# Layer 0's attention scores from rounded high and low parts of Q and K

## What is computed

```
aq, ak, av, bq, bk, bv = _split_even(hx @ w_in)          # tokens
caq, cak, cav, cbq, cbk, cbv = _split_even(hc @ w_in)    # context
aq = _apply_rope(aq, cos, sin);  ak = _apply_rope(ak, cos, sin)
ya = _window_attn(aq, ak, av, cak, cav, sink)            # band, and a sink
yb = _neighbourhood_attn(bq, bk, bv, cbk, cbv, rpb)      # bias table
y_c = concat([_ctx_attn(caq, cak, cav, sink), _ctx_attn(cbq, cbk, cbv, None)]) @ w_out
# each: s = (q . k) * 64 ** -0.5 (+ bias);  p = softmax(s);  out = p . v
```

## Time and profile before

| | us |
|---|---|
| median of 3 runs | 1332.49 |
| lowest, highest | 1331.76, 1337.83 |
| the profiled execution | 1336.08 |
| its span, first to last instruction | 1334.2 |

### The profile page before, as it was taken

The page is one execution under the profiler, slowest core; times in us unless marked ns, Lnnn a source line. Parts: engine busy times, 40 slices in busy tenths (PEclk is TensorE's granted clock), DMA queues, the critical chain, the costliest instruction groups (busy, mean ns, idle before and its releaser), DMA issues.

```text
span 1334.2 us, 25050 instructions
## 1 busy us (share of the span) xinstructions
PE 1298.1 (97%) x9434; PEld 1151.0 (86%) x9434; DVE 988.5 (74%) x1734; ACT 668.2 (50%) x1358; POOL 195.1 (15%) x268
## 2 busy tenths in 40 slices
PE   7999999999999999999999999999999999999997
PEld 6786779988888888898896899999999988999967
DVE  5698778999887878979428665655666886765884
ACT  4427743631523414344237664565465566465573
POOL 0101223000000000123104610000220016120043
PEclk8999999999999999999999999999999999999999
DMA  7774124366885867934320245655575443455511
GB/s 298 292 214 149 49 82 156 139 221 220 320 311 208 297 238 264 309 125 155 111 80 17 68 162 173 228 181 168 157 264 174 144 130 105 156 175 176 175 51 48
DMA packets 67665, 233.15 MB, mean 175 GB/s; under 512 B 7280, under 2 KB 12400, under 8 KB 67312
## 3 DMA queue, kind: packets, MB, share of 16 engines
q1 hardware_dynamic: 67568, 231.84, 51.6%
HBM read 230.76 MB, written 1.05 MB: 174 GB/s over the span
## 4 chain that ended last, share of the span: by engine, by line
PE 82%; DVE 7%; issue 3%; ACT 3%; POOL 2%; DMA 2%; SPq 0%; ACTq 0%; POOLq 0%; DVEq 0%
PE ps L1722 23%; PE ps L1723 23%; PE ps L1724 23%; PE ps L1947 4%; PE ps L1976 3%; PE ps L2007 2%; DVE wlo L969 2%; DMA aring<-aall 2%; POOL RS L1599 1%; PE ps L1991 1%; DVE ps L1043 1%; DVE ps L1006 1%; ACT whi L611 1%; DVE X L1389 1%; ACT wk L731 1%
## 5 line engine op out<-in xcount | busy, mean ns | idle before, releaser
L969 DVE TENSOR_TENSOR wlo<-raw,whi 128x1024 fp32r<-128x1024 f32 (+1 forms) x284 | 346.3, 1221 | 146.2 <-ACT whi L611 140.7
L611 ACT ACTIVATE whi<-raw 128x1024 fp32r<-128x1024 f32 (+1 forms) x284 | 296.5, 1045 | 262.7 <-PE ps L1724 260.5
L1722 PE MATMUL ps<-H,whi 128*128 128x256 f32 (+1 forms) x896 | 300.5, 335 | 3.9 <-DVE wlo L969 1.6
L1723 PE MATMUL ps<-H,whi 128*128 128x256 f32 (+1 forms) x896 | 296.9, 331 | 0.0
L1724 PE MATMUL ps<-H,wlo 128*128 128x256 f32 (+1 forms) x896 | 296.8, 331 | 0.0
L1722 PEld LDWEIGHTS ps<-H,whi 128*128 128x128 f32 x896 | 169.1, 189 | 24.3 <-issue 5.7
L1724 PEld LDWEIGHTS ps<-H,wlo 128*128 128x128 f32 x896 | 169.3, 189 | 16.9
L1723 PEld LDWEIGHTS ps<-H,whi 128*128 128x128 f32 x896 | 169.2, 189 | 16.1
L1722 PE MATMUL ps<-HID,whi 128*128 128x256 f32 (+1 forms) x536 | 175.3, 327 | 0.0
L1723 PE MATMUL ps<-HID,whi 128*128 128x256 f32 (+1 forms) x536 | 175.1, 327 | 0.0
L1724 PE MATMUL ps<-HID,wlo 128*128 128x256 f32 (+1 forms) x536 | 175.1, 327 | 0.0
(11 more groups left out here) (266 smaller groups left out, 2058.2 us busy)
## 6 DMA issues: line engine op xcount, KB each, us to landing
raw<-wall SPq DMA_DIRECT2D x270, 512.0 KB, 4.2
aring<-aall SPq DMA_DIRECT2D x144, 512.0 KB, 4.8
raw<-wall SPq DMA_DIRECT2D x14, 384.0 KB, 3.0
AL<-ali SPq DMA_DIRECT2D x14, 192.0 KB, 5.4
X<-xin SPq DMA_DIRECT2D x2, 1024.0 KB, 7.2
BI<-rpb SPq DMA_DIRECT2D x4, 512.0 KB, 9.2
out<-X SPq DMA_DIRECT2D x4, 256.0 KB, 2.4
cst<-const SPq DMA_DIRECT2D x1, 960.0 KB, 8.3
```

The costliest lines, as they stand in the source:

```text
L611: act.activation(whi[:, slot, 0:n], raw[:, slot, 0:n], ACT.Copy).then_inc(sem("w_hi"), 1)
L969: dve.tensor_tensor(wlo[:, slot, 0:n], raw[:, slot, 0:n], whi[:, slot, 0:n].bitcast(F32), ALU.subtract)\
L1722: pe.matmul(o, a[0], b[0], start=first, stop=False)
L1723: pe.matmul(o, a[0], b[1], start=False, stop=False)
```

## The change

`Q0` and `K0` become `Q2` and `K2`, with a rounded high and a rounded low part each (twice the bytes). All ten tiles are evacuated to one of four float32 staging tiles in `wk2`, the rotation writes there too. `l0_high` on ScalarE copies a finished tile into its high part, `l0_low` on VectorE subtracts the high part from the staged tile. The scores of layer 0 are three products (high by high, high by low, low by high), both heads in turn. Waits are added for both. The reserve for software DMA descriptors is set to 2048 bytes; no DMA of this kernel uses it.

```diff
         def l0_tile(i):
...
+            whole = wk2[:, i % 4, :]
+            if i <= 4:
+                return Tile(512, "q", whole[:, 0:N], whole[:, N:2 * N], 0.125 if i < 4 else 1.0)
+            return Tile(512, None, whole, None, 0.125 if i < 9 else 1.0)
...
@@ ScalarE
+            def l0_high(i):
+
+                if i <= 4:
+                    act.wait_ge(sem("rope_out"), i + 1)
+                act.wait_ge(sem("proj_out"), i + 1)
+                act.activation(l0_split(i, 0), wk2[:, i % 4, :], ACT.Copy).then_inc(sem("l0_high"), 1)
...
             evac(p_l0, FIRST - 1)
+            l0_high(0)
+            l0_high(1)
             for i in range(FIRST, L0_FM):
                 ahead(U_L0 + i)
+                act.wait_ge(sem("l0_low"), i - 3)
                 evac(p_l0, i)
+                l0_high(i - 2)
+            l0_high(L0_FM - 2)
+            l0_high(L0_FM - 1)
...
             exps(1)
+            act.wait_ge(sem("l0_low"), L0_FM)
             attend(*J_L0, begun=2)
...
@@ VectorE
+            def l0_low(i):
+
+                dve.wait_ge(sem("l0_high"), i + 1)
+                dve.tensor_tensor(l0_split(i, 1), wk2[:, i % 4, :], l0_split(i, 0).bitcast(F32), ALU.subtract)\
+                   .then_inc(sem("l0_low"), 1)
+
             for i in range(1, L0_FM):
                 steps(p_l0, i, i + 1)
                 ada_tiles(i)
+                if i >= 3:
+                    l0_low(i - 3)
             ahead(U_L0 + L0_FM)
+            l0_low(L0_FM - 3)
             ada_tiles(L0_FM)
+            l0_low(L0_FM - 2)
             maxima(0)
             ahead(U_L0 + L0_FM + 1)
+            l0_low(L0_FM - 1)
             ada_tiles(L0_FM + 1)
             maxima(1)
...
@@ TensorE
+                    if j.split:
+                        for of_q, of_k in ((0, 0), (0, 1), (1, 0)):
+                            for r in range(2):
+                                ins = pe.matmul(ps[:, 2 * (s % 2) + r, c0:c0 + nk], j.q(p, r, of_q), j.k(p, r, of_k),
+                                                start=of_q + of_k == 0, stop=of_q == 1)
+                        continue
...
-            pe.wait_ge(sem("rope_out"), 5)
+            pe.wait_ge(sem("l0_low"), 5)
             scores(0)
             scores(1)
             values(U_L0 + L0_FM, V_L0, 4, Hx[0], (1,))
             pe.wait_ge(sem("a_used"), ADA_EARLY + ADA_PROJ)
+            pe.wait_ge(sem("l0_low"), L0_FM)
             attend(*J_L0, begun=2, values_out=V_L0 + 4)
```

More of the change, by code:

```diff
@@ L178, in program @@
         s0 = ExitStack()
-        Q0 = sb("Q0", [P, 8, 2 * N], F32, s0)
-        K0 = sb("K0", [P, 2, 2 * N], F32, s0)
+        Q2 = sb("Q2", [P, 2, 8, 2 * N], F32R, s0)
+        K2 = sb("K2", [P, 2, 2, 2 * N], F32R, s0)
         V0 = sb("V0", [P, 4, N], F32, s0)
@@ L340, in l0_tile, with l0_split @@
         def l0_tile(i):
-            if i < 4:
-                return Tile(512, "q", Q0[:, i, 0:N], Q0[:, i, N:2 * N], 0.125)
-            if i == 4:
-                return Tile(512, "q", K0[:, 0, 0:N], K0[:, 0, N:2 * N])
-            if i < 9:
-                return Tile(512, None, Q0[:, i - 1, :], None, 0.125)
-            return Tile(512, None, K0[:, 1, :])
+            whole = wk2[:, i % 4, :]
+            if i <= 4:
+                return Tile(512, "q", whole[:, 0:N], whole[:, N:2 * N], 0.125 if i < 4 else 1.0)
+            return Tile(512, None, whole, None, 0.125 if i < 9 else 1.0)
+        def l0_split(i, part):
+            if i in (4, L0_FM - 1):
+                return K2[:, part, i // 5, :]
+            return Q2[:, part, i - i // 5, :]
         L1_SECOND = (range(0), range(0, 2), range(2, 4), range(4, 8)) + (range(0),) * (L1_FM - 4)
@@ L407, in __init__ @@
             def __init__(self, q, k, parts, bias, v, dst, b0=0, sink=None, diff=False, gate=None, tile=None,
-                         qr=None, kr=None):
+                         qr=None, kr=None, split=False):
                 self.q, self.k, self.bias, self.b0 = q, k, bias, b0
+                self.split = split
                 self.parts = [(sum(parts[:p]), nk) for p, nk in enumerate(parts)]
@@ L439, in program @@
                     jobs.append(Job(
-                        q=(lambda p, r, kind=kind, i=i, t=t: Q0[rows(r), 4 * kind + i, P * (t + p):P * (t + p) + P]),
-                        k=(lambda p, r, kind=kind, k0=k0: K0[rows(r), kind, k0:2 * N]),
+                        q=(lambda p, r, part, kind=kind, i=i, t=t: Q2[rows(r), part, 4 * kind + i, P * (t + p):P * (t + p) + P]),
+                        k=(lambda p, r, part, kind=kind, k0=k0: K2[rows(r), part, kind, k0:2 * N]), split=True,
                         parts=(N, N) if ctx_q else (2 * N,), bias=bias, b0=b0,
@@ L2398 @@
     assert arrays["wall"].shape == (UNITS, P, 1024) and arrays["aall"].shape == (ADA_UNITS, P, 1024)
-    nc = bacc.Bacc("TRN2", target_bir_lowering=False, num_devices=1)
+    nc = bacc.Bacc("TRN2", target_bir_lowering=False, num_devices=1, dynamic_dma_scratch_size=2048)
     args = [nc.dram_tensor(k, v.shape, mybir.dt.from_np(v.dtype), kind="ExternalInput").ap() for k, v in arrays.items()]
```

## The result

| | before | after |
|---|---|---|
| median | 1336.60 us (20 runs) | 1339.56 us (20 runs) |
| the profiled execution | 1336.08 | 1341.94 |
| its span | 1334.2 | 1340.0 |

One of before's 20 executions took 1612.54 us and has no part in the ratio. The ratio after to before is 1.0027, its interval 1.0017 to 1.0036: 2.3 to 4.8 us longer, 3.6 in the middle (the medians differ by 3.0), within the 0.5% that I called no change. A second measurement gave 1.0032 (1.0020 to 1.0044). What follows is about the terms of that sum: they were not all of the size that I gave them.

The account below looks back on a forecast made before the run. TensorE was taken to bound attention, with VectorE full before it. Entry +5.7, cheaper scores -3.6 and clock fall +1.6 gave +3.7 us on a median of 1332.49: 1336.2, range 1331 to 1342.

Parts of the forecast that it names:

- The entry, +5.7: Passage from projections to attention: ten VectorE subtractions of 0.61 us delay the maxima and the second transposes, +5.7 (5.3 to 6.5).
- Attention, -3.6: Scores 4 to 23: 20 jobs each save 0.18 us on TensorE, -3.6 (-4.2 to -3.3), with VectorE keeping up.
- The clock, +1.6: Entry to attention: TensorE's pauses drop its clock to half until about 116 us, +1.6 (0 to +3.5).
- scores 3 take 0.7 longer and half of what lies behind is lost: Half clock at the entry: scores 3 lengthen by 0.7 us and half the time from 114.3 to 116 or 117 is lost.
- The sum: Whole kernel: 5.7 - 3.6 + 1.6 = +3.7 us.
- A difference in the later stages: Behind attention: none was expected, and one would be a sign that the prediction was wrong.
- The base: Median of the kernel before, 1332.49 us, to which the forecast difference was added.
- Exposed weight loads: Rival, attention scores: each load waits for the matmul before it, 0.10 more a step; +9.7, 1342.2 us, chance 0.08.
- missing overlap: Rival, attention scores: half-height rounded pairs don't overlap, +0.50 a job, +17.3 in all; 1349.8 us, chance 0.04.
- Faster pairs: Rival, attention scores: rounded pairs run much faster than 0.227, so VectorE bounds; -1.1, 1331.4 us, chance 0.10.
- No fall of the clock: Rival, entry to attention: the clock does not fall in TensorE's pause; +2.1, 1334.6 us, chance 0.20.
- Waits forecast at nothing: Projections: evacuations on ScalarE wait for low parts because four staging tiles are shared; no cost, with 3 us of cover.

Follow-up runs that it names:

- filler: Changed kernel plus useless float32 products on TensorE, ten before its wait for the tenth low part and three before scores 3; ratio to the kernel before 1.0003.
- the second profile: The changed kernel measured and profiled once more, unchanged; ratio to the kernel before 1.0032 (1.0020 to 1.0044).

## Why the prediction was right, and where its terms were off

- **The entry, +5.7.** Right. The step that gave it (ten subtractions of 0.61 in front of the maxima) shows in the rows: maximum 0 at 104.9 on before's scale (forecast 105.0), maximum 1 done 110.2 (110.3), scores 3 at 112.4 (112.5), transposes 1 at 113.9 (113.7). Without the clock's fall scores 4 are 5.44 late (filler), inside the bounds of 5.3 to 6.5; with it 5.83. Removing the subtractions removes all of it, halving them takes off 2.3 at scores 2. That unit 7's high part comes just as VectorE wants it (forecast 64.5) was right too, and with nothing to spare: without the subtraction in front VectorE waits 0.45 for it.
- **Attention, -3.6.** It was -3.15, less than the lower bound of 3.3: 0.158 a job on the mean instead of 0.18. The pairs of rounded half-height products do overlap at 0.227 and 0.12, and the change from full to half height costs the 0.20 assumed. Two things are missing: the seven context jobs save 0.15, which I had only as a bound (my 0.92, measured 0.91) and left out of the sum; and VectorE's copy, which I found in time in a step of 3.14, is 0.06 late in one job of three of the band cycles.
- **The clock, +1.6.** The fall came, where forecast, and lasted to 110.8 (113.7 on before's scale; forecast 116). Its price was 0.4, and 0.1 in the second profile. The failed step is "scores 3 take 0.7 longer and half of what lies behind is lost": the work at half clock lay mostly in time in which TensorE waited for VectorE and ScalarE. The forecast took the same microseconds twice, once as waiting and once as slow work.
- **The sum.** 5.44 - 3.15 + 0.39 = 2.68, the lateness in the profile, against +3.7 forecast and 3.6 (2.3 to 4.8) measured over the whole. That the forecast met the measured difference to 0.1 is partly luck: the clock term was too much by 1.2, the entry by 0.3 and the saving by 0.4, which together put the forecast 1.0 above the lateness at attention's end, and either noise or the time behind attention made up for the rest. A difference in the later stages I had named as a sign of being wrong; it came in this pair of profiles (6 us), and before shows it against itself.
- **The base.** The forecast stood on a median of three runs; over 20 runs it is 4.1 us higher. The range of 1331 to 1342 held the 1339.56 by its width on the slow side, which was meant for other cases.
- **The rivals.** Exposed weight loads and missing overlap: no, scores are 0.89 to 0.95, not 1.09 or 1.56 (for a context job I had 1.40; 0.92 and five times 0.10 are 1.42). Faster pairs: no. No fall of the clock: it fell, but at +0.4 the two cases lie together.
- **Waits forecast at nothing.** ScalarE's evacuations did wait for the subtractions (by 5.2 us at 85.2), and TensorE didn't notice: its last value product starts at +46.0 from unit 4 (100.23), +46.3 before.

## What to carry to other kernels

Where an engine has no idle time ahead of a hand-over, work that is added to it comes out at the hand-over in full, at its step from start to start, however early it is placed; what it saves elsewhere must be set against that, and here ten subtractions (5.4) cost more than 20 jobs with cheaper products gave (3.15). Before a fall of the clock is priced, ask what the engine would have waited for at full clock: only the work on the path costs. And a median of three runs or a single pair of profiles can't carry a difference of 3 us in 1336: a kernel against itself made 5 in the profile and 0.1% in the ratio.

## What the runs showed of the hardware that I had not expected

- A GpSimd elementwise operation with two inputs lengthens VectorE's neighbouring instruction by 0.88 us (1.28 to 2.16), one with one input by 0.17; GpSimd's own takes up to 2.2 or 2.4 beside VectorE, and 1.3 at best. Moving an operation from VectorE to GpSimd made VectorE slower.
- Half-height products of two heads run in pairs in either order of the code, 0.89 and 0.90 us a job.
- The granted clock falls at places behind attention in some executions of the same kernel and not in others, 3.4 us of it costing 0.6 to 1.6. Two profiles of the kernel before are 5.1 us apart, 2.2 by such a fall, 2.9 by rounded products that step by 0.118 instead of 0.113 us at a clock of 1.00.
- A fall of 6.8 us at the entry cost 0.1, 0.4 and some 0.9 us, with TensorE busy for 3.40, 4.90 and 5.99 of them.
